# Expert weights as one 8 KB run per partition, with stride-2 stationary operands

## The reference, cut to what matters

```python
cap = CAPACITY_FACTOR * seq // N_EXPERTS                      # 64
aff = softmax(einsum('bsd,de->bse', h, w_router))
gate, idx = lax.top_k(aff.transpose(0, 2, 1), cap)
xe = h[idx]                                                   # rows of each expert
a = silu(einsum('becd,edf->becf', xe, w_gate)) * einsum('becd,edf->becf', xe, w_up)
ye = einsum('becf,efd->becd', a, w_down) * gate
y = zeros.at[idx].add(ye)
```

## Time and profile before

| | us |
|---|---|
| median of 3 executions | 1732.81 |
| lowest and highest | 1731.86 and 1734.91 |
| span of the profiled execution, first to last instruction | 1732.2 |
| TensorE matmul, busy | 1569.3 (91%) |
| TensorE weight load, busy | 1006.7 (58%) |
| VectorE, busy | 574.1 (33%) |
| ScalarE, busy | 474.7 (27%) |
| DMA moved | 305.15 MB |

### The profile page before, as it was taken

How to read it: one execution, slowest core, us unless ns; L and a number is a source line. 1 busy time by engine, 2 the same in 40 slices (tenths; PEclk the granted TensorE clock), 3 DMA queues, 4 the chain that set the end, 5 groups by cost and what they waited for, 6 DMA issues and landing times.

```text
span 1732.2 us, 18849 instructions
## 1 busy us (share of the span) xinstructions
PE 1569.3 (91%) x7428; PEld 1006.7 (58%) x7428; DVE 574.1 (33%) x1061; ACT 474.7 (27%) x855; POOL 100.6 (6%) x118
## 2 busy tenths in 40 slices
PE   6959959988499999999999789998989899999998
PEld 3434526633234434434434479996767688888886
DVE  0145365442401211211211462112556433344334
ACT  2143236611211011011101331124763433213321
POOL 2000030000000000000000120000002211000100
PEclk9979969998799999999999899998989999999999
DMA  5279360012199999999999302214011132233221
GB/s 204 30 247 380 125 230 1 2 60 75 49 402 380 384 408 377 387 405 393 387 408 381 120 25 73 74 50 146 1 37 49 49 97 98 97 98 97 98 73 49
DMA packets 105457, 305.15 MB, mean 176 GB/s; under 512 B 7052, under 2 KB 43173, under 8 KB 103346
## 3 DMA queue, kind: packets, MB, share of 16 engines
q1 hardware_dynamic: 104712, 304.14, 47.0%
q0 software_dynamic: 512, 0.09, 0.1%
q10 hardware_dynamic: 170, 0.05, 0.0%
HBM read 300.07 MB, written 4.19 MB: 176 GB/s over the span
## 4 chain that ended last, share of the span: by engine, by line
PE 83%; DVE 6%; ACT 4%; POOL 2%; DMA 2%; issue 1%; SPq 1%; ACTq 0%; DVEq 0%; POOLq 0%
PE ps L683 19%; PE ps L725 11%; PE ps L726 11%; PE ps L727 11%; PE ps L448 4%; PE ps L671 4%; PE ps L613 3%; PE ps L713 3%; PE ps L809 2%; PE ps L566 2%; ACT sb L946 2%; PE ps L574 2%; DMA sb<-in_w_mod 2%; PE ps L489 1%; PE ps L589 1%
## 5 line engine op out<-in xcount | busy, mean ns | idle before, releaser
L683 PE MATMUL ps<-sb 128*64 128x512 f32 x1536 | 334.9, 594 | 13.3 <-ACT sb L946 13.3
L683 PEld LDWEIGHTS ps<-sb 128*64 128x64 f32 x1536 | 110.1, 137 | 221.7 <-issue 214.3
L946 ACT ACTIVATE sb<-ps 128x512 f32<-128x512 f32 (+5 forms) x217 | 104.3, 485 | 423.1 <-PE ps L683 163.9
L725 PE MATMUL ps<-r_act,r_top 128*128 128x512 f32 x352 | 138.3, 393 | 3.5 <-POOL r_act L1885 2.3
L727 PE MATMUL ps<-r_act,r_low 128*128 128x512 f32 x352 | 137.3, 390 | 0.0
L1759 DVE TENSOR_TENSOR r_low<-raw,r_top 128x2048 fp32r<-128x2048 f32 x33 | 74.4, 2293 | 79.9 <-ACT r_top L946 79.9
L1582 DVE TENSOR_TENSOR sb<-sb,ps 128x512 f32<-128x512 f32 x16 | 11.0, 688 | 253.5 <-PE ps L683 253.5
L726 PE MATMUL ps<-r_low,r_mid 128*128 128x512 f32 x240 | 93.4, 389 | 0.0
L725 PE MATMUL ps<-r_low,r_h 128*128 128x256 f32 x320 | 90.7, 283 | 0.0
L726 PE MATMUL ps<-r_low,r_h 128*128 128x256 f32 x320 | 90.6, 283 | 0.0
L727 PE MATMUL ps<-r_low,r_top 128*128 128x256 f32 x288 | 81.5, 283 | 0.0
(11 more groups left out here) (353 smaller groups left out, 2393.4 us busy)
## 6 DMA issues: line engine op xcount, KB each, us to landing
sb<-in_w_gate SPq DMA_DIRECT2D x64, 1024.0 KB, 17.9
sb<-in_w_up SPq DMA_DIRECT2D x64, 1024.0 KB, 11.2
sb<-in_w_down SPq DMA_DIRECT2D x64, 1024.0 KB, 12.6
sb<-in_w_mod SPq DMA_DIRECT2D x16, 1536.0 KB, 9.4
raw<-in_f_w_up SPq DMA_DIRECT2D x22, 1024.0 KB, 7.7
raw<-in_a_w_in SPq DMA_DIRECT2D x12, 1024.0 KB, 5.4
raw<-in_f_w_down SPq DMA_DIRECT2D x5, 2048.0 KB, 7.7
sb<-in_w_in SPq DMA_DIRECT2D x4, 1440.0 KB, 10.6
```

The source lines that it names most:

```text
L683: mm = pe.matmul(PS[64 * hf:64 * hf + 64, b * HALF:(b + 1) * HALF], lhsT(k), ring[:, c % RINGN, kk, hf * HALF:(hf + 1) * HALF], start=(k = ...
L725: pe.matmul(o, a_hi, b_hi, start=first, stop=False)
L946: return act_(o, i_, ACT.Identity, bias=bias, scale=scale)
```

## The change

The rows of a chunk are dealt out otherwise. Partition p of chunk c now holds contraction rows 256 c + 2p (j = 0) and 256 c + 2p + 1 (j = 1), which lie side by side in DRAM. The other operand must have its channels in the same order: block k of xeT takes from h2 every second column, beginning at 256 (k // 2) + k % 2 within a half, and the transposes of act do the same. Copies, buffers, semaphores and the order of issue are unchanged.

```diff
@@ gather (L671)
-    mm = pe.matmul(bank(6 + j)[:, k * P:(k + 1) * P], h2[:, t, (4 * j + k) * P:(4 * j + k + 1) * P],
+    mm = pe.matmul(bank(6 + j)[:, k * P:(k + 1) * P], h2[:, t, 512 * j + 256 * (k // 2) + k % 2:512 * j + 256 * (k // 2) + 256:2],
                    onehot[:, t, :], start=(t == 0), stop=(t == NT - 1), skip_group_check=True)
@@ turn_act (L692)
-    tr = pe.transpose(bank(b)[:, fb * P:(fb + 1) * P], act[:, e, fb * P:(fb + 1) * P], ident)
+    tr = pe.transpose(bank(b)[:, fb * P:(fb + 1) * P], act[:, e, 256 * (fb // 2) + fb % 2:256 * (fb // 2) + 256:2], ident)
@@ SP's part (L1918)
-    gate = [I[n].rearrange("a e (c j p) f -> (a e) c p j f", p=P, j=2) for n in ("w_gate", "w_up", "w_down")]
+    gate = [I[n].rearrange("a e (c p j) f -> (a e) c p j f", p=P, j=2) for n in ("w_gate", "w_up", "w_down")]
```

## The result

| | us |
|---|---|
| before, median of 7 (1729.03 to 1734.91) | 1732.81 |
| after, median of 7 (1734.93 to 1740.33) | 1736.81 |
| ratio | 1.003, 95% interval 1.0018 to 1.0043 |
| profiled execution of after, time and span | 1740.33 and 1738.5 |

The change made the kernel slower by 0.3%: the medians are 4.0 us apart, and the interval of the ratio comes to 3.1 to 7.5 us. No change was forecast. 1736.8 lies in the range given, but the sign is that of a case with a chance of 0.18.

A forecast was written before the change was run, and what follows sets the result against it. TensorE was taken to bound the expert stage, at 64.50 us a pair. The sum, 0 (load) + 0 (gather) + 0 (transposes), left the span at 1732.2 us and the forecast at 1732.8 us, range 1728 to 1746.

The forecast's parts named there:

- a case with a chance of 0.18: Kernel slower: full stride price 0.08, partial stride price 0.06 and slower transfers 0.04 together.
- The bound: Expert stage: TensorE sets the pace at 64.50 us a pair; no wait for a load is on the chain.
- The load at 0: Expert-weight DMAs with 8 KB runs: a small rate gain, hidden behind TensorE, so 0 us.
- The gather at 0: Gathering matmuls (L671), 512 stationary loads at every second column: cost taken as 0, bounds 0 to 54 us.
- the nearest row: Broadcast stationary load (L792): 205 ns against 190 contiguous, 15 ns more; with 9 ns hidden, 3 us for the gather.
- The transposes at 0: Transposes of act (L692), 64 instructions at every second column: cost taken as 0, bounds 0 to 7 us.
- At the same bounds: Transposes priced with the gather's bounds per load, 0 to 106 ns, giving 0 to 7 us.
- a lost exemption: The one later pair whose gather has no clock drop gets one: +1.6 us.
- The slower rivals: Strided stationary loads, full price 1787 to 1794 us or partial, and slower transfers, 1742 to 1749 us; together chance 0.18.
- The full stride price: Gather and transposes: strided stationary loads at half pace, 54 to 61 us more, 1787 to 1794 us; chance 0.08.
- The milder form: Gather: a stationary load dearer by a quarter (27 ns) gives 9 us, 1742 us; chance 0.06.
- Its point of decision: Gather: the milder stride price decides from about 16 ns extra per load.

The follow-up runs named there:

- The load alone: Kernel before with only the new load of one 8 KB run per partition, TensorE operands contiguous: 1732.29 us, ratio 1.0002.
- gather alone: Kernel before with only the gather's stationary operand at every second column, loads and transposes as before: 1737.00 us, ratio 1.0032.
- the version with contiguous operands: The change with VectorE writing h2 and act even columns first, weights loaded to match, so TensorE's operands are contiguous: 1732.82 us, ratio 1.0005.
- two more transposes: Kernel before with the last transpose of act done three times instead of once, nothing strided: 1737.78 us, ratio 1.0043.
- the transposes alone: Kernel before with only the transposes of act at every second column, loads and gather as before: 1733.7 us, ratio 1.0008.
- a filler: Kernel before with one unused 512-column matmul more at the top of TensorE's loop: 1723.39 us, ratio 0.9954.
- the changed kernel with a filler: The changed kernel with one unused 512-column matmul more at the top of TensorE's loop: 1732.31 us, ratio 1.0002 to the kernel before.

## Why the prediction was wrong

**The bound, right.** TensorE paces the loop and no load is on the chain. The load alone left the time and the loop as they were.

**The load at 0, right,** with a gain of the rate smaller than its upper bound: 422 GB/s in full windows and 2.7% where it binds, 436 or 6% assumed. It fell into a longer dry stretch.

**The gather at 0: the step that failed.** The true price is 0.30 us in a pair with a drop and 0.39 in one without, 2.4 to 3.1 us over eight pairs. The prediction had the bound, the nearest row and a cover of "about 9 ns (115 - 106) in which a dearer load would hide". The cover was wrong. The 115 is 7.36/64 and contains the entry and the exit of the stage; load after load goes at 111 to 112 ns. And the pace of the load was taken from the durations of two line groups, 106 ns for 128 columns, from which its pace at a step of two cannot be had: it is 117. From the sum itself 512 x (nearest row 15 - 9) = 3 us was the value to take for an unmeasured pattern on the bounding engine, and I took 0 in its stead. That it would have come so near is luck: the row is a broadcast load, which no run ties to a step of two, and the 9 ns of cover in it were not there.

**The transposes at 0: also failed.** They cost 0.09 us for four, 1.4 us in all. "At the same bounds" passed over that a transpose's load is another kind: 140 ns for 128 columns where a matmul's is 190. It became 68 ns longer, where the spacing of the gather's loads grew by 6 ns; why, no run shows.

**The clock.** The prediction priced a lost exemption at 1.6 us and said that "the timing before the gather is untouched". What is before the gather is the whole previous pair, and when it gets longer the drop falls elsewhere in the gather. With 64.50 us one or two of the seven later pairs were free of the drop in each of three profiles; with 64.65 to 64.97 none was in any of four. In two of the profiles, gather alone and whole change, this and the first gather account for what the operands do not.

The clock records of the traces show how the drop moves. Its start is given here from the first load of each gather. Before, with pairs of 64.50 us, it is 0.1, 0.4, 0.8 and 1.2 us in the second to fifth pair, the sixth has no drop, and then it is 0.1 and 0.4 again. The load alone gives the same series, and the version with contiguous operands also goes from 0.1 to 1.2 between its two free pairs. After the change, with 64.97 us, it goes slowly back, from 1.3 to 0.6 over the seven pairs, and with two more transposes from 1.2 to 0.8. With the transposes alone it goes forward, from -0.3 to 0.9, and with the gather alone from -0.4 to 0.3. In these seven profiles a free pair among the later ones comes right after a drop at 1.1 or 1.2 us (or it is the second pair), and none of the four kernels with longer pairs went up past that place. So it seems to matter where the drop stands and how fast it moves, and a longer pair need not lose the free one. This is a pattern and not a cause that was tested. It doesn't say why a filler removes the drops, and in the changed kernel with a filler the first free pair comes after a drop at 0.7 us.

How much of it is in the medians, and not in the profiles only, can be read from the mean granted clock of every execution: twice its distance from 1, times the span, is the time at half clock. It is 165 us on average for before (34 executions, standard error 1), 165 for the load alone and for the transposes alone (2), 174 for the gather alone (2) and 169 for the change (1.5). Other sets of before have 162 to 164. A gather with a drop loses 1.62 us by some 3.4 us at half clock, so a microsecond at half clock costs about half a microsecond where TensorE is busy, and less where it waits. An estimate from these numbers: the clock is up to 4 or 5 us of the difference for the gather alone, up to 2 to 3.5 us for the change, and about nothing for the transposes alone, although their profile had no free pair.

Together: 3.8 us of operands (8 x 0.48) and some clock, for a measured difference of 4.0 us (3.1 to 7.5). That the operands cost this is shown by the chain; how the rest is split between the gathers and other places at half clock stays open. What makes a gather miss the drop was not settled either; the run of the change with a filler shows that the gap alone does not decide.

**The slower rivals.** The full stride price (54 to 61 us) is near what a step of four costs, 59.7, and not a step of two; that the two agree so well is luck, since 52.6 of the 59.8 us of the loop are operands and the rest mostly clock. The milder form was the true one, below the 9 us that it was priced at. Its point of decision, 16 ns a load, was too high, since it counted the 9 ns of cover and the gather alone.

## What to carry to other kernels

A transfer that is busy all the time may still not be the bound; ask the waits of the compute engine, and halve its work if you want to see the transfer's own rate. Where the transfer is off the chain, an edit that pays for it with a dearer operand on the bounding engine is a loss however small the operand's price is. So price the operand at its nearest row and not at zero, and count several hundred instructions. Where the layout is needed, have it made by an engine that has time, as VectorE here, where it cost nothing that could be measured.

## What the runs showed of the hardware

- A float32 stationary load of 128 columns for a matmul passes every 117 to 119 ns at a step of two words and every 233 at a step of four; contiguous loads come every 111 to 112. At half clock the spacing is 213 contiguous and at a step of two, and stays 233 at a step of four.
- A transpose's load of 128 columns takes 140 ns contiguous and 208 to 209 at a step of two or four alike.
- VectorE's instruction that writes 1024 float32 values by turns into two runs takes 2011 ns instead of 1285, of 512 from PSUM 1072 instead of 688.
- One run of 8 KB per partition instead of two of 4 KB gives 421 GB/s for 410 where the loads set the pace.
- One 512-column matmul placed in a gap of 0.98 us went with seven of seven later gathers at full clock, in place of one of seven, and was worth 7.9 us; in the changed kernel five of seven were. In the kernel before, the filler took the time at half clock from 163 to 148 us on average (12 and 5 executions).
